# State-space groups: the products of the new inputs go ahead of the scaling of the former group's outputs, and the low part of those outputs goes to the end of its slot

## The chip, the cores and the metric

The kernel runs on one core of one Trainium2 chip. The metric is the device time of one execution in microseconds. TensorE (PE) multiplies matrices, VectorE (DVE) and ScalarE (ACT) work elementwise, GpSimd (POOL) helps, and SyncE (SP) issues the loads of weights.

## The reference, cut to what matters

A model of six layers on 256 tokens of 2048 numbers: four layers of attention and recurrence, then a state-space layer and a layer of dilated attention. Only the state-space layer (`_ssd_mixer`) is touched by the change. Its computation:

```python
z, xBC, dt = split(h @ in_w)
xBC = silu(causal_conv4(xBC) + conv_b)          # xs, B, C come out of this
dt = softplus(dt + dt_bias)
cb = C . B over the state, per group            # 8 groups of 8 heads of 64
decay = exp(acum_l - acum_s), causal
y_diag = (cb * decay) @ (xs * dt)
y = (y_diag + xs * D_skip) * silu(z)
y = y * rsqrt(mean(y*y over the group) + eps) * norm_g
out = y @ out_w                                  # 4096 -> 2048
```

There is one chunk of 256 tokens, so no state is carried from chunk to chunk.

## The kernel before, in words

**Products in three parts.** All values lie in SBUF with features on the 128 partitions and the 256 tokens along the free axis. Each fp32 weight is split into a high and a low part: ACT writes `w_hi` (line 1026), DVE writes `w_lo = w_raw - w_hi` (line 1594), and PE adds three products (lines 446 to 448). A load of weights is a *slot* of 16 blocks of 128x128, split in two halves of 1024 columns. There are two buffers of split weights, so the work of slot n on ACT and DVE (`hi_ahead`, `lo_half`) prepares the weights of slot n+2 in the buffer that PE frees half by half in slot n. PE writes its tiles to two banks in turn: a tile can start once DVE has taken the last tile but one (`tile_taken`).

**Groups.** `s_group(g)` runs 10 slots for each of the 8 groups, one tile each: slots 0 and 1 give B and C, slots 2 to 5 the four pairs of heads' inputs xs, and slots 6 to 9 the four tiles of z. After groups 2 and 4 comes a projection (`s_project`, 8 slots of two half-length tiles each), and after group 7 a third projection with `tail=True`, then the last one. Each engine's queue is written out by hand in this order; there is no planner, and each engine executes its own list in order, waiting on semaphores.

**What happens in a slot of a group.** DVE: low half 0, take the tile (line 2166), low half 1, then a piece of the former group (`s_previous`), in slots 4 to 7 the inputs of one pair (`s_inputs`: one product with D, line 2116, then four products of the turned tile with dt, line 2121, which release `turn_read`), then the convolution (slots 0 to 5, lines 2093 to 2096) and the clamp for the sigmoid (line 2103). ACT: high half 0, decays of a pair in slots 8, 9, 2 and 3 (`s_decay`, lines 1367 and 1370), high half 1, the sigmoid of the last slot's tile (lines 1070 to 1072), its piece of the former group, and in slot 7 two fetches of rows for the decays (`s_fetch`, line 1359, a DMA). POOL: the product with the sigmoid (line 2504), and the decays' product with cb (`s_weights`, lines 2511 and 2512), which releases `m_ready`. PE: the tile, then the former group's output product (`s_out`, lines 812 and 813, in slots 0, 1, 3 and 4, which waits for `m_ready` and for DVE's reading of the last one, lines 2109 and 2110), and in slots 4 to 7 the turn of a pair (`turn`, line 485, into one bank, which waits for `turn_read` of the last turn).

**The former group's outputs.** The four tiles of y are made in slots 0, 1, 3 and 4 (`s_y_out`), their squares are summed, the factor comes in slot 5, and in slot 6 DVE scales the four tiles (`s_scale_y`, line 2129). ACT then writes their high part (`s_y_hi`, line 1375) as the last thing of its slot 6, and DVE the low part (`s_y_lo`, line 2136) at the start of its slot 7. Only the projections read these.

Of the kernel before, what the change touches and what calls it, by code (L numbers as in the profile page):

```python
# [192 lines left out]
def _program(nc, ctx, t, counts):  # L193
# [91 lines left out]
    def K(name, n=None, rows=P):  # L285
        a = CON[name]
        w = dict(CONST_PARTS)[name] if n is None else n
        return con[0:rows, a:a + w]
# [1293 lines left out]
    def _(dve):  # L1582
# [6 lines left out]
        def lo_half(half, ahead=2):  # L1589

            k = c.k["slot"] + ahead - 1
            cols = slice(half * HALF, (half + 1) * HALF)
            dve.wait_ge(hi_ready, c.at("slot", ahead) * 2 + (half - 1) if half == 0 else c.at("slot", ahead) * 2)
            dve.tensor_tensor(w_lo[k % SPLIT][:, cols], raw[MAIN_AT[k] % RAW][:, cols], w_hi[k % SPLIT][:, cols], SUB).then_inc(lo_ready, 1)  # L1594

        def begin():

            c.next("slot")
            lo_half(0)
# [33 lines left out]
        def take(columns=False):  # L1633
            if columns:
                q = c.next("mod") - 1
                dve.wait_ge(ada_done, q + 1)
            dve.wait_ge(tile_done, c.next("tile"))
            g = G[c.bank][:, 0:SEQ]
            if columns:
                add = vec[:, VEC["ada_b"] + 2 * q:VEC["ada_b"] + 2 * q + 2]  # L1640
                dve.tensor_tensor(mod[:, 2 * q:2 * q + 2], G[c.bank][:, SEQ:SEQ + 2], add, ADD).then_inc(mod_done, 1)
            c.bank ^= 1
            return g
# [437 lines left out]
        def s_conv(g, n):  # L2081

            xb = s_xbp[:, n % 2]
            if n < 2:
                dst = s_bc[n]
                dve.wait_ge(cb_done, c.at("cb"))
                at = 32 + 8 * n + g
            else:
                dst = s_xv[n % 2]
                at = 4 * g + n - 2  # L2090
            dve.wait_ge(tile_taken, c.at("tile"))
            w = lambda k: V("s_conv_w", 48 * k + at)
            link(dve.tensor_scalar(dst, xb[:, 0:SEQ], w(0), V("s_conv_b", at), MUL, ADD))
            for k in (1, 2):
                link(dve.scalar_tensor_tensor(dst, xb[:, k:k + SEQ], w(k), dst, MUL, ADD))  # L2095
            link(dve.scalar_tensor_tensor(dst, xb[:, 3:3 + SEQ], w(3), dst, MUL, ADD))
            s_clamp(n, dst)

        def s_clamp(n, src):

            dve.wait_ge(gluon, c.at("glued", -1))
            c.next("glued")
            dve.tensor_scalar(s_zc[n % 2], src, SIG_MIN, None, MAX).then_inc(clamped, 1)

        def s_y_out(g, m):

            dve.wait_ge(yd_done, c.next("yd"))
            dve.wait_ge(gluon, 10 * g + 7 + m)
            link(dve.tensor_tensor(s_y[:, m], bO[:, 0:SEQ], s_dx[:, m], ADD))
            dve.tensor_tensor(s_y[:, m], s_y[:, m], s_z[:, m], MUL).then_inc(s_y_ready, 1)  # L2110

        def s_inputs(g, m):

            dve.wait_ge(gluon, c.next("gluon", 3 if m == 0 else 1))
            dve.wait_ge(s_y_ready, c.at("yd"))
            link(dve.tensor_scalar(s_dx[:, m], s_xv[m % 2], V("s_D", 4 * g + m), None, MUL))
            dve.wait_ge(turn_done, c.next("turn"))
            for b in range(2):
                for hh in range(2):
                    head = 8 * g + 2 * m + hh  # L2120
                    last = dve.tensor_scalar(s_xdt[:, b, m, 64 * hh:64 * hh + 64], bT[:, b * P + 64 * hh:b * P + 64 * hh + 64],  # L2121
                                             s_tok[:, b, head:head + 1], None, MUL)
            last.then_inc(turn_read, 1)

        def s_scale_y(g):

            factor()
            for m in range(4):
                last = dve.scalar_tensor_tensor(s_y[:, m], s_y[:, m], V("s_norm_g", 4 * g + m), rsn[:, 2], MUL, MUL)  # L2129
            last.then_inc(y_ready, 1)  # L2130
            dve.wait_ge(y_ready, c.next("y"))

        def s_y_lo(g):
            dve.wait_ge(x_hi, c.next("x"))
            four = slice(4 * (g % 4), 4 * (g % 4) + 4)
            dve.tensor_tensor(q_lo[:, four], s_y, q_hi[:, four], SUB).then_inc(x_lo, 1)

        def s_previous(g, step):
            if step in S_OUT:
                s_y_out(g, S_OUT.index(step))  # L2140
            if step == 6:
                s_scale_y(g)

        def s_steps(n):

            if n == 0:
                softplus_sum(s_y[:, 0], s_y[:, 1])
            if n == 1:
                softplus_end(s_dt[:], s_y[:, 0], s_y[:, 1], s_y[:, 2], s_y[:, 3], s_dt[:])
                link(dve.tensor_scalar(s_y[:, 0], s_dt[:], tiny[:, 0:1], -1.0, MUL, MUL))  # L2150
                link(dve.memset(s_y[:, 1], 1.0))
                dve.tensor_tensor_scan(s_ac[:], s_y[:, 1], s_y[:, 0], 0.0, MUL, ADD).then_inc(dt_ready, 1)
            if n == 4:
                dve.wait_ge(turn_done, c.next("turn"))
                dve.tensor_copy(s_tok.rearrange("p a b -> p (a b)"), bT[:]).then_inc(turn_read, 1)
                dve.wait_ge(turn_read, c.at("turn"))

        def s_group(g):
            for n in range(10):
                if g and n == 7:  # L2160
                    s_y_lo(g - 1)
                begin()
                if g == 0:
                    s_steps(n)
                x = take(columns=n == 1 and g in (3, 5))
                dve.tensor_copy(s_xbp[:, n % 2, 3:3 + SEQ] if n < 6 else s_z[:, n - 6], x).then_inc(tile_taken, 1)
                lo_half(1)
                if g:
                    s_previous(g - 1, n)
                if 4 <= n <= 7:  # L2170
                    s_inputs(g, n - 4)
                if n < 6:
                    s_conv(g, n)
                else:
                    dve.wait_ge(tile_taken, c.at("tile"))
                    s_clamp(n, s_z[:, n - 6])
                if n == 7:
                    dve.wait_ge(cb_done, c.next("cb"))
                    dve.tensor_tensor(s_cb[:, 0:P], bS[0][:, 0:P], K("causal"), MUL)
                    dve.tensor_copy(s_cb[:, P:SEQ], bS[0][:, P:SEQ])  # L2180
                    dve.tensor_tensor(s_cb[:, SEQ:384], bS[0][:, SEQ:384], K("causal"), MUL).then_inc(cb_read, 1)
            c.next("gluon", 4)
# [49 lines left out]
        def layer_s():  # L2232
            c.k["turn"] = 2 * 3 * A_HEADS + 3 * B_PAIRS
            dve.wait_ge(x_lo, c.at("x"))
            dve.sem_inc(mod_x, 1)
            link(dve.memset(s_xbp[:, :, 0:3], 0.0))

            begin()
            g = take()
            dve.tensor_scalar(s_dt[:], g, V("s_dt_bias"), None, ADD).then_inc(tile_taken, 1)  # L2240
            lo_half(1)
            dve.wait_ge(tile_taken, c.at("tile"))
            c.next("soft")
            softplus_begin(s_dt[:], s_y[:, 1])
            for g in range(S_GROUPS):
                s_group(g)
                if g in (2, 4):
                    s_project(g // 2 - 1)
            s_project(S_PAIRS - 2, tail=True)
            scale, gain = mod[:, 64:80], vec[:, VEC["ln_g"]:VEC["ln_g"] + DT]  # L2250
            dve.tensor_tensor(ln_a, gain, scale, MUL)
            link(dve.tensor_tensor(ln_b, vec[:, VEC["ln_b"]:VEC["ln_b"] + DT], scale, MUL))
            link(dve.tensor_tensor(ln_b, ln_b, mod[:, 48:64], ADD))
            s_project(S_PAIRS - 1)
            layer_norm(0)
# [544 lines left out]
```

## Time and profile before

| | us |
|---|---|
| median of 3 runs (3546.73 to 3554.34) | 3548.98 |
| profiled execution, its own time | 3549.42 |
| profiled execution, its span | 3547.6 |
| PE busy | 3447.0 (97%) |
| DVE busy | 2783.1 (78%) |
| ACT busy | 1987.5 (56%) |
| POOL busy | 587.2 (17%) |
| mean granted clock of TensorE | 0.995 |

The profiled execution is one run on the chip, recorded. A row of the timeline gives the start in us from the span's start, the length in us, the engine and line, the operation, and in brackets how long the engine had been idle before and what released it. Instructions of one line that follow one another are merged (x4), and their starts can overlap the end of the one before by some 0.09 us. The state-space layer lies between about 2216 and 2920 us. The rows below are mostly of group 3, whose slot 7 has its turn at 2507.30 on PE, and of group 4, which follows it directly. Groups 1 and 2, 3 and 4, and 5, 6 and 7 follow one another directly; the projections stand after groups 2, 4 and 7.

### The profile page before, as it was taken

The page shows a single profiled execution, that of the slowest core. Times are in us where ns is not written, and L with a number is a line of the kernel's source. Part 1 is how long each engine was busy: PE and PEld are TensorE (multiplying, and loading weights), DVE is VectorE, ACT ScalarE, POOL GpSimd, SP SyncE. Part 2 cuts the span into 40 slices and gives each one's busy share as a digit, 9 for nine tenths or more (in the row PEclk, how much of TensorE's full clock was granted, in tenths as well). Part 3 has the DMA queues.
Part 4 walks back from the last instruction along what each step waited for, and adds up shares of the span by engine and source line. Part 5 has one row for each costly group of instructions (what it writes and reads, how often), then busy time and mean ns, then how long its engine had stood idle before and what let it go on. Part 6 is the DMA issues. An engine that isn't in the chain of part 4 may idle for free.

```text
span 3547.6 us, 68240 instructions
## 1 busy us (share of the span) xinstructions
PE 3447.0 (97%) x27858; PEld 3381.8 (95%) x27858; DVE 2783.1 (78%) x4529; ACT 1987.5 (56%) x3204; POOL 587.2 (17%) x546
## 2 busy tenths in 40 slices
PE   7999999999999999999999999999999998999997
PEld 7999999999999998999999999999999998999997
DVE  7788888577797887877888887898989867666665
ACT  6555546566547676565555546665656746434344
POOL 2111112111113011131111112231313300000000
PEclk9999999999999999999999999999999999999999
DMA  6555556444465444655555565556464543555552
GB/s 239 217 197 219 217 227 231 176 155 179 165 251 203 172 169 173 267 185 218 201 221 202 208 262 180 178 175 230 171 233 169 186 169 146 210 189 199 204 190 107
DMA packets 113688, 699.61 MB, mean 197 GB/s; under 512 B 13216, under 2 KB 29792, under 8 KB 31456
## 3 DMA queue, kind: packets, MB, share of 16 engines
q1 hardware_dynamic: 104128, 685.14, 52.2%
q10 hardware_dynamic: 8784, 8.46, 1.0%
q8 instruction: 222, 3.64, 0.4%
q0 software_dynamic: 464, 1.64, 0.1%
q14 instruction: 90, 0.74, 0.1%
HBM read 684.64 MB, written 2.16 MB: 194 GB/s over the span
## 4 chain that ended last, share of the span: by engine, by line
PE 49%; DVE 13%; ACT 6%; issue 2%; DMA 1%; POOL 1%; DVEq 0%; SPq 0%; POOLq 0%; ACTq 0%
PE g L446 15%; PE g L448 15%; PE g L447 15%; DVE w_lo L1594 4%; ACT w_hi L1026 2%; DMA w_raw<-in_slots 1%; POOL scratch L2409 1%; DVE vec L2095 1%; DVE rstd L2095 1%; PE turn_bank L485 1%; DVE scratch L1659 1%; DVE scratch L2121 0%; DVE scratch L2129 0%; PE norm_bank L459 0%; DVE h L2225 0%
## 5 line engine op out<-in xcount | busy, mean ns | idle before, releaser
L1594 DVE TENSOR_TENSOR w_lo<-w_raw,w_hi 128x1024 fp32r<-128x1024 f32 x1088 | 1337.0, 1232 | 433.9 <-ACT w_hi L1026 423.1
L1026 ACT ACTIVATE w_hi<-w_raw 128x1024 fp32r<-128x1024 f32 x1088 | 1129.6, 1053 | 873.2 <-PE g L448 761.7
L446 PE MATMUL g<-p_hi,w_hi 128*128 128x256 f32 x4576 | 1318.0, 288 | 36.4 <-DVE w_lo L1594 23.2
L448 PE MATMUL g<-p_hi,w_lo 128*128 128x256 f32 x4576 | 1296.2, 283 | 0.0
L447 PE MATMUL g<-p_lo,w_hi 128*128 128x256 f32 x4576 | 1296.2, 283 | 0.0
L446 PE MATMUL g<-q_hi,w_hi 128*128 128x256 f32 x3408 | 980.0, 288 | 5.7 <-DVE w_lo L1594 2.2
L448 PE MATMUL g<-q_hi,w_lo 128*128 128x256 f32 x3408 | 964.0, 283 | 0.0
L447 PE MATMUL g<-q_lo,w_hi 128*128 128x256 f32 x3408 | 963.8, 283 | 0.0
L446 PEld LDWEIGHTS g<-p_hi,w_hi 128*128 128x128 f32 x4576 | 879.1, 192 | 46.1 <-DVE w_lo L1594 32.7
L447 PEld LDWEIGHTS g<-p_lo,w_hi 128*128 128x128 f32 x4576 | 879.3, 192 | 1.4
L448 PEld LDWEIGHTS g<-p_hi,w_lo 128*128 128x128 f32 x4576 | 879.0, 192 | 0.0
L446 PEld LDWEIGHTS g<-q_hi,w_hi 128*128 128x128 f32 x3408 | 653.1, 192 | 9.6 <-issue 3.5
L447 PEld LDWEIGHTS g<-q_lo,w_hi 128*128 128x128 f32 x3408 | 653.4, 192 | 1.1
L448 PEld LDWEIGHTS g<-q_hi,w_lo 128*128 128x128 f32 x3408 | 653.0, 192 | 0.0
L2409 POOL TENSOR_SCALAR scratch<-scratch 128x256 f32<-128x256 f32 x112 | 149.9, 1339 | 473.9 <-DVE scratch L1702 259.6
L2394 POOL TENSOR_TENSOR acc<-acc,sq 128x256 f32<-128x256 f32 x120 | 114.6, 955 | 306.5 <-ACT sq L1055 304.4
L1659 DVE SCALAR_TENSOR_TENSOR scratch<-w_raw,tiny,scratch 128x256 f32<-128x256 f32 x312 | 154.1, 494 | 8.6
L1070 ACT ACTIVATE scratch<-scratch 128x256 f32<-128x256 f32 x152 | 63.0, 414 | 166.4 <-POOL scratch L2409 165.0
L2449 POOL TENSOR_TENSOR scratch<-scratch,cos_a 128x256 f32<-128x256 f32 x64 | 52.6, 822 | 585.2 <-DVE scratch L1796 585.2
L1659 DVE SCALAR_TENSOR_TENSOR acc<-w_raw,tiny,acc 128x256 f32<-128x256 f32 x260 | 136.4, 525 | 7.1
L446 PE MATMUL g<-c_hi,w_hi 128*128 128x256 f32 x336 | 100.2, 298 | 0.4 <-DVE h L2186 0.4
L448 PE MATMUL g<-c_hi,w_lo 128*128 128x256 f32 x336 | 95.8, 285 | 0.0
(445 smaller groups left out, 3929.2 us busy)
## 6 DMA issues: line engine op xcount, KB each, us to landing
w_raw<-in_slots SPq DMA_DIRECT2D x640, 1024.0 KB, 4.9
scratch<-scratch SPq DMA_DIRECT2D x128, 64.0 KB, 4.9
scratch<-s_rows ACTq DMA_DIRECT2D x16, 256.0 KB, 3.4
con<-s_rows ACTq DMA_DIRECT2D x16, 256.0 KB, 5.1
h<-in_x SPq DMA_DIRECT2D x4, 512.0 KB, 6.2
out_h<-h SPq DMA_DIRECT2D x4, 512.0 KB, 2.6
sq<-in_p POOLq DMA_DIRECT2D x4, 256.0 KB, 3.0
con<-in_consts SPq DMA_DIRECT2D x1, 832.0 KB, 10.7
```

Source lines behind the costliest of these rows:

```text
L446: pe.matmul(g, wh, hi[:, k], start=n == 0, stop=False)
L447: pe.matmul(g, wh, lo[:, k], start=False, stop=False)
L448: last = pe.matmul(g, wl, hi[:, k], start=False, stop=n == len(ks) - 1)
L485: last = pe.transpose(bT[:, n * P:(n + 1) * P], s, K("ident"))
L1026: act.activation(w_hi[k % SPLIT][:, cols], raw[MAIN_AT[k] % RAW][:, cols], ACT.Copy).then_inc(hi_ready, 1)
L1070: link(act.activation(buf, buf, ACT.Exp, scale=-1.0))
L1594: dve.tensor_tensor(w_lo[k % SPLIT][:, cols], raw[MAIN_AT[k] % RAW][:, cols], w_hi[k % SPLIT][:, cols], SUB).then_inc(lo_ready, 1)
L1659: link(dve.scalar_tensor_tensor(a, w, s, a, MUL, ADD))
L2095: link(dve.scalar_tensor_tensor(dst, xb[:, k:k + SEQ], w(k), dst, MUL, ADD))
L2394: pool.tensor_tensor(acc[:], acc[:], sq[:, j % 2], ADD).then_inc(summed, 1)
L2409: pool.tensor_scalar(dst, src, SIG_MIN, None, MAX).then_inc(clamped, 1)
L2449: pool.tensor_tensor(t2[:, n % 2], qn[:, n % 2], cos_a[:], MUL).then_inc(cos_done, 1)
```

## The change

In the slots of groups 1 to 7 (where there is a former group):

- In slot 6 DVE runs the inputs of the third pair (`s_inputs`, 5 instructions) and the clamp first, and then the scaling of the former group's four tiles (`s_scale_y`).
- In slot 7 the low part (`s_y_lo`) is no longer before DVE's low half 0, but behind the clamp of the slot, ahead of the reading of the cb product.

In slots 0 to 5 the order is as before. The third projection (tail), ACT, POOL, PE and SP keep their lists.

```diff
         def s_group(g):
             for n in range(10):
-                if g and n == 7:
-                    s_y_lo(g - 1)
                 begin()
                 if g == 0:
                     s_steps(n)
                 x = take(columns=n == 1 and g in (3, 5))
                 dve.tensor_copy(s_xbp[:, n % 2, 3:3 + SEQ] if n < 6 else s_z[:, n - 6], x).then_inc(tile_taken, 1)
                 lo_half(1)
-                if g:
+                if g and n < 6:
                     s_previous(g - 1, n)
                 if 4 <= n <= 7:
                     s_inputs(g, n - 4)
...
                 else:
                     dve.wait_ge(tile_taken, c.at("tile"))
                     s_clamp(n, s_z[:, n - 6])
+                if g and n > 5:
+                    s_previous(g - 1, n)
+                if g and n == 7:
+                    s_y_lo(g - 1)
                 if n == 7:
                     dve.wait_ge(cb_done, c.next("cb"))
```

## Rows read from the trace of the kernel before

**Rows 1.** The waits of PE from 2200 to 2900: us in total, times, longest.
```profile
PE turn_bank L485 <- DVE scratch L2121: 9.6, 7, 1.4
PE out_bank L812 <- POOL scratch L2512: 3.0, 7, 0.8
```

**Rows 2.** The timeline of PE at slot 7 of group 3 and slot 3 of group 4.
```profile
2507.30 0.44 PE L485 MATMUL turn_bank<-con,vec 128*128 128x128 f32 x2 [1.37 <-DVE scratch L2121]
...
2545.28 0.66 PE L812 MATMUL out_bank<-scratch 128*64 128x256 f32 x4 [0.36 <-POOL scratch L2512]
```

**Rows 3.** The timeline of DVE, slots 5 to 8 of group 3.
```profile
2497.34 0.84 DVE L2116 TENSOR_SCALAR scratch<-vec 128x256 f32<-128x256 f32 x1
...
2503.80 2.16 DVE L2129 SCALAR_TENSOR_TENSOR scratch<-scratch,vec,rsn 128x256 f32<-128x256 f32 x4
2505.99 0.35 DVE L2116 TENSOR_SCALAR scratch<-rstd,vec 128x256 f32<-128x256 f32 x1
2506.38 0.86 DVE L2121 TENSOR_SCALAR scratch<-turn_bank,scratch 128x64 f32<-128x64 f32 x4
2507.16 0.28 DVE L2103 TENSOR_SCALAR scratch<-scratch 128x256 f32<-128x256 f32 x1
2507.36 1.22 DVE L2136 TENSOR_TENSOR q_lo<-scratch,q_hi 128x1024 fp32r<-128x1024 f32 x1
...
2516.62 1.23 DVE L1594 TENSOR_TENSOR w_lo<-w_raw,w_hi 128x1024 fp32r<-128x1024 f32 x1 [1.53 <-ACT w_hi L1026]
```

**Rows 4.** The scaling in the third projection, on DVE.
```profile
2875.86 1.67 DVE L2129 SCALAR_TENSOR_TENSOR scratch<-scratch,vec,rsn 128x256 f32<-128x256 f32 x4
```

**Rows 5.** The timeline of POOL in slot 6 of group 3.
```profile
2502.72 1.77 POOL L2504 TENSOR_TENSOR vec<-vec,sin_b 128x256 f32<-128x256 f32 x1 [4.69 <-ACT sin_b L1072]
```

**Rows 6.** The timeline of ACT, slots 6 to 8 of group 3, slots 0 to 2 of group 4.
```profile
2505.99 1.06 ACT L1375 ACTIVATE q_hi<-scratch 128x1024 fp32r<-128x1024 f32 x1 [3.35 <-DVE scratch L2129]
2506.96 1.99 ACT L1026 ACTIVATE w_hi<-w_raw 128x1024 fp32r<-128x1024 f32 x2
2509.74 0.37 ACTq L1359 DMA_DIRECT2D scratch<-s_rows  x1
...
2513.12 1.64 ACT L1367 ACTIVATE scratch<-scratch 128x128 f32<-128x128 f32 x4 [0.76 <-DMA scratch<-s_rows]
...
2524.81 1.99 ACT L1026 ACTIVATE w_hi<-w_raw 128x1024 fp32r<-128x1024 f32 x2
...
2535.84 0.42 ACT L1383 ACTIVATE rsn<-scratch 128x256 f32<-128x256 f32 x1 [1.13 <-DVE scratch L2110]
2536.32 1.06 ACT L1026 ACTIVATE w_hi<-w_raw 128x1024 fp32r<-128x1024 f32 x1
```

**Rows 7.** The timeline of DVE in slots 1 and 2 of group 4.
```profile
2533.54 1.23 DVE L1594 TENSOR_TENSOR w_lo<-w_raw,w_hi 128x1024 fp32r<-128x1024 f32 x1 [0.18 <-ACT w_hi L1026]
...
2540.77 1.23 DVE L1594 TENSOR_TENSOR w_lo<-w_raw,w_hi 128x1024 fp32r<-128x1024 f32 x1 [0.91 <-ACT w_hi L1026]
```

**Rows 8.** The timeline of DVE, slot 1 of groups 2, 6 and 7.
```profile
2355.54 1.23 DVE L1594 TENSOR_TENSOR w_lo<-w_raw,w_hi 128x1024 fp32r<-128x1024 f32 x1 [0.40 <-ACT w_hi L1026]
...
2711.61 1.23 DVE L1594 TENSOR_TENSOR w_lo<-w_raw,w_hi 128x1024 fp32r<-128x1024 f32 x1 [0.35 <-ACT w_hi L1026]
...
2777.08 1.23 DVE L1594 TENSOR_TENSOR w_lo<-w_raw,w_hi 128x1024 fp32r<-128x1024 f32 x1
```

**Rows 9.** DVE, then PE, at the third tile of the first projection.
```profile
2418.23 0.48 DVE L2186 SCALAR_TENSOR_TENSOR h<-g,mod,h 128x256 f32<-128x256 f32 x1
...
2418.61 0.28 PE L448 MATMUL g<-q_hi,w_lo 128*128 128x256 f32 x1
2418.86 0.36 PE L446 MATMUL g<-q_hi,w_hi 128*128 128x256 f32 x1
```

**Rows 10.** DVE, then PE, at the second tile of the third projection.
```profile
2835.96 0.47 DVE L2186 SCALAR_TENSOR_TENSOR h<-g,mod,h 128x256 f32<-128x256 f32 x1
...
2838.37 0.28 PE L446 MATMUL g<-q_hi,w_hi 128*128 128x256 f32 x1
```

## The prediction

> **What bounds the kernel now.** I read the busy shares first (PE 97%, DVE 78%, ACT 56%): PE sets the time, so an edit on DVE counts by what it does to PE's waits. Second, PE's waits in the state-space layer. Seven times, once in each of groups 1 to 7, the turn of slot 7 waits 1.37 us for DVE's products of slot 6, 9.6 us in all; seven more waits, 3.0 us, are for POOL's weights [rows 1]. Third, the timelines of the four engines around slot 7 of group 3. PE had its tile done at 2507.30 - 1.37 = 2505.93 and stood until L2121 ended at 2506.38 + 0.86 = 2507.24 [rows 2, 3]. DVE's list shows why: the scaling (L2129, 2.16 us) stands ahead of L2116 and L2121 [rows 3]. This is the wait that the change can take away.
>
> Fourth, who waits for the scaling. ACT's high part of y (L1375) stands idle 3.35 us for it, and behind it in ACT's queue lie the two high halves of slot 7, the sigmoid and the fetch of the rows at 2509.74 [rows 6]. The rows land at 2513.12, 3.38 us later, and ACT waits 0.76 us for them before the decays. From there to the pair of high halves that starts at 2524.81 ACT is all but always busy. DVE waits for ACT in slot 8 (1.53 us) and again in slots 1 and 2 of group 4 (0.18 and 0.91) [rows 3, 6, 7]. In slot 1 its output tile (L2110) releases ACT's square at 2535.84, behind which come the high half, the decays of pair 2 and the sigmoid; POOL's weights follow, and PE waits 0.36 us for them at 2545.28 [rows 2, 6]. After 2540.77 DVE has no wait until slot 8 of group 4. So end of scaling, fetch, decays, DVE in slots 0 and 1, ACT and DVE in slot 2, DVE to the next scaling form a ring with almost no slack, beside PE. That ring is the second bound, and the scaling's end lies on it.
>
> **The wait that goes.** After the change L2116 starts at 2503.80, where the scaling did. There it meets POOL's product (2502.72, 1.77 us) [rows 5]. In slot 5 the same instruction in the same position behind the low half took 0.84 us, against 0.35 in slot 6 [rows 3]. I take 0.84 + 0.03 to the next start. L2121 ends at 2503.80 + 0.87 + 0.86 = 2505.53, ahead of PE's 2505.93: the wait goes whole, 1.36 us a group (7 of them, 9.6).
>
> **The scaling's end.** L2116 0.87, four L2121 0.78 (2506.38 to 2507.16), the clamp 0.20 (to 2507.36), then four scalings. These took 2.16 us behind the low half but 1.67 in the third projection, where POOL runs nothing [rows 3, 4]; I take 1.67, since POOL's product is then over. The end moves from 2505.96 to 2503.80 + 3.52 = 2507.32: **s = 1.36 us later**. Bounds: nothing blocked, 0.39 + 0.78 + 0.20 + 1.67 - 2.16 = 0.88; both blocked, 1.85. The block of 0.49 moves from the scaling (2.16 - 1.67) to L2116 (0.84 - 0.35), so the middle value is the one that the rows fit.
>
> The Trainium skill, SBUF — State Buffer, "Who interferes with whom", says that a DVE instruction in a 2-port mode or with two SBUF inputs and a GpSimd one exclude each other for a whole instruction, whichever starts second. The trace agrees in kind (0.84 against 0.35). By that rule exactly one instruction pays, as in the middle value; without it s would be 0.88 and the sum below 2.5.
>
> **The low part of y.** L2136 (1.22 us) leaves the start of slot 7. Nothing on PE waits for it until a projection, more than two slots later. But DVE's low half 0 can't start at about 2508.5 any more: it needs ACT's high half, which now ends at 2506.96 + 1.36 + 1.04 = 2509.36, so DVE idles about 2.0 us and is 0.9 late. With L2136 behind the clamp (1.13) and up to 0.3 for a POOL product that L2116 of slot 7 now meets earlier, DVE is 2.3 us later at the second half of slot 8. It had idled 1.53 (1.6 with the overlap of starts) and ACT delivers 1.36 later, so 3.0 us are free [rows 3, 6]: the cover holds with 0.6 us to spare. PE's slots 8 and 9 need nothing earlier than that. So this half of the change costs nothing; if the cover goes, each further 0.1 us goes into the ring.
>
> **The lag, ring by ring.** ACT's high part, high halves, sigmoid and fetch all come s later; the fetch is issued at 2511.1 and lands at 2514.5. From there ACT, POOL and DVE carry s into slots 8, 9 and the next group. What absorbs it in a next group: the wait of DVE in slot 1 plus 0.09 of overlap, 0.49, 0.27, 0.44 and 0.09 for groups 2, 4, 6 and 7 [rows 7, 8] (in group 7 the low half has no wait before it), and ACT's gap between square and high half, 2536.32 against 2536.26 - 0.09, 0.15 [rows 6]. Together k = 0.65, 0.43, 0.59, 0.24. So PE, which waits for POOL's weights in slot 3 already, is there s - k later than before, although it comes 1.36 earlier: the wait grows from 0.36 to about 2.5 us and the gain is spent. Slot 7 then gives 1.36 back, but the ring is now s - k late, and the next scaling adds s once more.
>
> At a projection the lag reaches PE another way. Its fifth tile waits until DVE has taken the third: DVE takes it at 2418.23 to 2418.71, PE goes on at 2418.86, 0.13 behind its pitch [rows 9]. DVE has no wait between ACT's late high halves and this one, so PE takes over the whole lag there. It is the same after group 4. In the third projection DVE takes the second tile until 2836.43 and PE starts the fourth at 2838.37; less 0.15 from release to start, 1.8 us are free [rows 10]. Behind it DVE waits for PE several times, so nothing more is handed on.
>
> **The sum.** Groups 1 and 2 with the first projection: 2s - 0.65 = 2.07. Groups 3 and 4 with the second: 2s - 0.43 = 2.29. Groups 5, 6 and 7 with the third: 3s - 0.59 - 0.24 - 1.8 = 1.45. The removed waits are in this: these are PE's positions, and wherever PE waits for the ring its own earlier gain no longer counts. The sum is 7s - 3.71 = **+5.8 us**: 3549.42 + 5.8 = 3555.2 for an execution like the profiled one (span 3553.4), and 3554.8 against the median 3548.98, 0.44 below the profiled execution. With s = 0.88 it is +2.5, with 1.85 +9.2.
>
> **The rivals.**
> (a) *The wait goes and the lag is hidden*: -9.6 us, 3539.4. For it: PE is the 97% engine, and ACT and DVE show idle time in slot 8. Against it: that idle time is the ring's own (the rows' landing, then ACT), and is not there in slots 2 to 7. It needs 1.36 us of slack in the ring in each group; I find 0.24 to 0.65. 12%.
> (b) *The rings within the groups hold, but the projections swallow the lag*: PE leaves group 2 at 0.71 - 1.36 = -0.65, group 4 at -0.43, and the tail at +1.45, as above: +0.4, 3549.4. Against it is PE's late fifth tile [rows 9], a small wait of 0.13 us that might be something else. 16%.
> (c) *DVE itself becomes the bound in slots 7 and 8*: POOL's product, now 1.36 us later, blocks L2116 of slot 7 for most of its length, 1.1 us more than I take instead of the 0.6 to spare. Then 0.5 us more enter the ring in each of 7 groups, +3.5: 3558.3. It decides from an L2116 of 1.4 us on; the longest wait of this kind in these rows is 0.49. 12%.
>
> **The numbers.** My forecast has 60%, with (a) 12, (b) 16 and (c) 12. Within 0.2% (7.1 us; about what a measurement of this kernel can tell from no change) lie 3541.9 to 3556.1. My forecast is within but near the upper end; a quarter of its chance, 15, lies above it (s over 1.54, or less absorbed). So faster 12%, same 61% (45 + 16), slower 27% (15 + 12). The range 3546.5 to 3558.8 leaves out (a) and part of (c); my case alone has 3551.5 to 3558.2 from its bounds of s.
>
> **What would show it.** In the changed profile: PE's wait at L485 for L2121 gone in all seven groups; ACT's wait at L1375 3.35 + 1.36 = 4.7 us; PE's wait at L812 for POOL unchanged in groups 1, 3 and 5 and 2.4 to 2.9 us in groups 2, 4, 6 and 7; PE's wait for DVE's taking at the fifth tile of the first two projections about 2.9 us each (0.13 + 2.07 + 0.65, and 0.13 + 2.29 + 0.43); group 3's first slot 2.1 us later than now and group 5's 4.4. L812 waits that stay at 0.36 would prove me wrong at the ring, absent waits at L2186 at the projections, and a DVE that never waits for ACT in slot 8 would mean (c).

## The result and the profile after

The changed kernel takes 3555.59 us (median of 13 runs, 3553.19 to 3559.02) against 3548.87 of the kernel before (13 runs): +6.7 us, ratio 1.002 with a 95% interval of 1.0013 to 1.0027. Forecast were 3554.8 and +5.8. The profiled execution has a span of 3557.2 us. From the start of the last turn of dt in group 0 to the first matrix product of the layer norm behind the projections, the state-space layer took 2908.1 - 2237.6 = 670.5 us before and 2916.7 - 2240.0 = 676.7 after: 6.2 us more. The rest of the difference of the two spans (3.4 us) lies outside what the change touches.

PE's waits in the layer, us in total, times, longest:

```profile
PE out_bank L812 <- POOL scratch L2514: 9.7, 7, 2.3
PE g L446 <- DVE scratch L2164: 4.2, 3, 1.5
PE g L446 <- DVE h L2188: 3.2, 5, 1.1
...
PE out_bank L812 <- DVE scratch L2110: 1.0, 2, 0.9
```

The turn's wait of 9.6 us [rows 1] is gone: no row for L485 and L2121 is left. In its place the wait for POOL's weights grew from 3.0 to 9.7, and two waits for DVE's taking of tiles came: 4.2 us, and 3.2 where it had been 1.1. With 1.0 for DVE's output tile that is 14.0 us more and 9.6 less, 4.4 net. The remainder up to 6.2 is hardly idle time. For about 1.5 us it is TensorE's clock, which fell once in the layer, right behind the wait of 2.26 us in slot 3 of group 6. Each row gives a stretch, its length, the busy time of PE, PEld (the loading of weights), DVE, ACT and POOL, the granted clock, the DMA share and GB/s:

```profile
2720.00:2730.90 10.90, 8.65 (x73) 8.44 (x71) 9.87 (x15) 9.03 (x18) 5.43 (x5) 1.00 0.53 182
2730.90:2735.00 4.10, 4.10 (x23) 3.66 (x24) 4.03 (x8) 2.17 (x6) 1.82 (x2) 0.58 0.22 92
2735.00:2740.00 5.00, 5.00 (x44) 4.57 (x44) 4.86 (x7) 2.21 (x3) 2.71 (x3) 1.00 0.59 213
```

From 2732 to 2734 the granted clock is 0.50 (1.2 of 2.4 GHz). From the output product of slot 3 to that of slot 4 PE needs 2739.13 - 2730.90 = 8.23 us, against 2730.10 - 2723.35 = 6.75 before, 1.48 more. The waits of 2.23 and 2.25 us in groups 2 and 4 had no such fall behind them.

DVE in slot 6 and the start of slot 7 of group 3, then slot 8:

```profile
2508.27 0.83 DVE L2116 TENSOR_SCALAR scratch<-rstd,vec 128x256 f32<-128x256 f32 x1
2509.14 0.86 DVE L2121 TENSOR_SCALAR scratch<-turn_bank,scratch 128x64 f32<-128x64 f32 x4
2509.92 0.28 DVE L2103 TENSOR_SCALAR scratch<-scratch 128x256 f32<-128x256 f32 x1
2510.12 1.67 DVE L2129 SCALAR_TENSOR_TENSOR scratch<-scratch,vec,rsn 128x256 f32<-128x256 f32 x4
2513.92 1.22 DVE L1594 TENSOR_TENSOR w_lo<-w_raw,w_hi 128x1024 fp32r<-128x1024 f32 x1 [2.14 <-ACT w_hi L1026]
...
2522.97 1.23 DVE L1594 TENSOR_TENSOR w_lo<-w_raw,w_hi 128x1024 fp32r<-128x1024 f32 x1 [1.32 <-ACT w_hi L1026]
```

From the start of this piece to the scaling's end it is 2511.79 - 2508.27 = 3.52 us, against 2.16 before [rows 3]: the end is 1.36 us later, to the hundredth the s of the prediction. L2116 took 0.83 and the four scalings 1.67. DVE then idles 2.14 us for the high half, and in slot 8 it still waits for ACT (1.32), so it is not itself the bound there.

ACT in slots 6 to 8 of group 3:

```profile
2511.81 1.06 ACT L1375 ACTIVATE q_hi<-scratch 128x1024 fp32r<-128x1024 f32 x1 [4.71 <-DVE scratch L2129]
2512.78 1.99 ACT L1026 ACTIVATE w_hi<-w_raw 128x1024 fp32r<-128x1024 f32 x2
...
2515.56 0.37 ACTq L1359 DMA_DIRECT2D scratch<-s_rows  x1
...
2519.48 1.64 ACT L1367 ACTIVATE scratch<-scratch 128x128 f32<-128x128 f32 x4 [1.86 <-DMA scratch<-s_rows]
```

The high part waits 4.71 us where it had waited 3.35 [rows 6], and the chain behind it is the same. This fetch took 3.92 us to land instead of 3.38, so the decays begin half a us later than s alone would have it. Group 3 is the extreme: over groups 1 to 7 this landing took 3.10 to 3.92 us, against 3.13 to 3.55 before.

PE from slot 3 of group 2 on, waits for POOL, for DVE's output tile, and the new ones at the first projection:

```profile
2370.17 0.66 PE L812 MATMUL out_bank<-scratch 128*64 128x256 f32 x4 [2.23 <-POOL scratch L2514]
2413.08 0.39 PE L446 MATMUL g<-q_hi,w_hi 128*128 128x256 f32 x1 [1.54 <-DVE scratch L2164]
2419.61 0.39 PE L446 MATMUL g<-q_hi,w_hi 128*128 128x256 f32 x1 [0.42 <-DVE h L2188]
2423.33 0.36 PE L446 MATMUL g<-q_hi,w_hi 128*128 128x256 f32 x1 [0.58 <-DVE h L2188]
2484.28 0.66 PE L812 MATMUL out_bank<-scratch 128*64 128x256 f32 x4 [0.36 <-POOL scratch L2514]
2536.17 0.66 PE L812 MATMUL out_bank<-con,scratch 128*64 128x256 f32 x4 [0.88 <-DVE scratch L2110]
2550.99 0.66 PE L812 MATMUL out_bank<-scratch 128*64 128x256 f32 x4 [2.25 <-POOL scratch L2514]
...
2730.90 0.66 PE L812 MATMUL out_bank<-scratch 128*64 128x256 f32 x4 [2.26 <-POOL scratch L2514]
2797.30 0.66 PE L812 MATMUL out_bank<-scratch 128*64 128x256 f32 x4 [1.40 <-POOL scratch L2514]
```

Read it as a pattern: after a projection (2484.28, group 3) the wait is the old 0.36; in a group that directly follows another it is 1.4 to 2.3. From slot 3 of group 3 to slot 3 of group 4 PE needs 2550.99 - 2484.28 = 66.71 us. Before it was 65.46, so this group became 1.25 us longer although a wait of 1.37 had been taken out of it. It is the largest case: from group 1 to 2, 5 to 6 and 6 to 7 it is 65.88, 66.01 and 66.40, 0.4 to 0.9 longer.

### The profile page after: what moved, and what is told of

Read it like the earlier page. It is cut to its first block, busy times and chain, and to the rows that moved or that the text cites. A ratio compares the mean times of both kernels' runs of the same rounds, so it can differ in the third digit from the quotient of the medians.

```text
span 3557.2 us, 68247 instructions
## 1 busy us (share of the span) xinstructions
PE 3453.3 (97%) x27858; PEld 3389.3 (95%) x27858; DVE 2781.8 (78%) x4529; ACT 1985.4 (56%) x3204; POOL 586.4 (16%) x546
## 3 DMA queue, kind: packets, MB, share of 16 engines
HBM read 684.64 MB, written 2.16 MB: 193 GB/s over the span
## 4 chain that ended last, share of the span: by engine, by line
PE 44%; DVE 14%; ACT 8%; issue 3%; DMA 2%; POOL 1%; ACTq 0%; DVEq 0%; SPq 0%; POOLq 0%
PE g L446 13%; PE g L448 13%; PE g L447 13%; DVE w_lo L1594 5%; ACT w_hi L1026 3%; DMA w_raw<-in_slots 1%; DMA scratch<-s_rows 1%; POOL scratch L2411 1%; ACT scratch L1367 1%; DVE vec L2095 1%; DVE rstd L2095 1%; DVE scratch L1659 1%; PE turn_bank L485 1%; DVE scratch L2121 0%; DVE scratch L2164 0%
## 5 line engine op out<-in xcount | busy, mean ns | idle before, releaser
L446 PE MATMUL g<-q_hi,w_hi 128*128 128x256 f32 x3408 | 982.5, 288 | 11.5 <-DVE scratch L2164 4.2
```

The lines of the kernel that those rows point to most:

```text
L446: pe.matmul(g, wh, hi[:, k], start=n == 0, stop=False)
```

## The experiments

Each is timed against the kernel before in five rounds; changes in us are the difference of the medians, with the ratio's 95% interval. The changed kernel is called "after". The edits of experiments 1, 2, 5, 6, 7 and 9 are shown against the kernel before, those of 3, 4 and 8 against after.

**1. Only the scaling moved.** The low part of y stays at the start of slot 7.

```diff
-                if g:
+                if g and n < 6:
                     s_previous(g - 1, n)
...
                     s_clamp(n, s_z[:, n - 6])
+                if g and n > 5:
+                    s_previous(g - 1, n)
```

> Only the order of slot 6 is changed (inputs and clamp ahead of the scaling); the low part of y is at the start of slot 7 as before. My theory (a ring from the end of the scaling over ScalarE, the fetch of the rows, the decays and VectorE back to the next scaling, 1.36 us longer): the whole effect is in this half, +5 to +7 us against the kernel before, the wait of the turn in slot 7 gone, the waits for GpSimd's weights in slot 3 of groups 2, 4, 6 about 2.2 us. Rival (the moved low part of y makes VectorE late in slots 7 and 8, and that is the loss): -9.6 us here, since the turn's wait is gone and nothing else is added.

Measured: 3556.18 against 3549.67, +6.5 us, ratio 1.002 (1.0011 to 1.0029). PE's waits for POOL's weights are 10.4 us in seven, longest 2.3, and the turn's wait is gone. The whole loss is in this half.

**2. Only the low part moved.** Slot 6 is as before.

```diff
-                if g and n == 7:
-                    s_y_lo(g - 1)
                 begin()
...
                     s_clamp(n, s_z[:, n - 6])
+                if g and n == 7:
+                    s_y_lo(g - 1)
```

> Only the low part of y is moved behind the clamp of slot 7; slot 6 is as before. My theory: no change, -1 to +1 us; the turn's wait of 1.37 us stays in seven groups and VectorE idles a little more in front of its low half in slot 7 and less in slot 8. Rival (the low part's new place costs): +5 us or more.

Measured: 3547.90 against 3549.67, -1.8 us, ratio 0.9996 (0.9988 to 1.0005): not to be told from no change. The turn's wait is 9.5 us. The rival with the low part falls.

**3. After, with ACT's high part behind the fetch.** DVE's list is that of after.

```diff
-            if step == 6:
+            if step == 6 and g == S_GROUPS - 1:
                 s_y_hi(g)
...
                 if n == 7:
                     s_fetch(g, 0)
                     s_fetch(g, 1)
+                    if g:
+                        s_y_hi(g - 1)
```

> The changed kernel, and ScalarE's high part of y (which waits for the scaling) goes from the end of its slot 6 to the end of slot 7, behind the sigmoid and the fetch of the rows, for groups 1 to 7. The scaling's end is then off the ring. My theory: the gain of the turn's wait comes back whole, -8 to -10 us against the kernel before (about 15 faster than the changed kernel), the waits for GpSimd's weights in slot 3 back to about 0.4 us. Rival (VectorE's own list or its contention with GpSimd is what got longer): stays at +4 to +7 us, since VectorE's list is that of the changed kernel.

Measured: 3538.21 against 3549.67, -11.5 us, ratio 0.9971 (0.9960 to 0.9981), a little more than expected. It is 18 us under experiment 1 with the same slot 6 on DVE, so DVE's own list was not what cost. PE's waits in the layer, then its slot 3 in groups 3 and 4:

```profile
PE out_bank L812 <- POOL scratch L2516: 3.4, 7, 1.3
...
PE g L446 <- DVE h L2190: 1.1, 1, 1.1
```

```profile
2477.51 0.66 PE L812 MATMUL out_bank<-scratch 128*64 128x256 f32 x4 [0.36 <-POOL scratch L2516]
2541.40 0.66 PE L812 MATMUL out_bank<-scratch 128*64 128x256 f32 x4 [0.37 <-POOL scratch L2516]
```

Neither the turn's wait nor the new ones are there, and a group takes 63.89 us, 1.57 under the kernel before. I call the ring open here: the scaling's end no longer holds up ACT's high halves, the fetch and the decays, so it no longer leads back to itself. ACT in slots 7 and 8 of group 3 shows it:

```profile
2505.53 0.37 ACTq L1359 DMA_DIRECT2D scratch<-s_rows  x1
2505.94 0.48 ACTq L1359 DMA_DIRECT2D con<-s_rows  x1
2506.47 1.06 ACT L1375 ACTIVATE q_hi<-scratch 128x1024 fp32r<-128x1024 f32 x1 [0.52 <-issue]
...
2508.72 1.64 ACT L1367 ACTIVATE scratch<-scratch 128x128 f32<-128x128 f32 x4 [0.24 <-DMA scratch<-s_rows]
```

The high part waits for nothing but its place behind the fetch, and the decays wait 0.24 us instead of 1.86.

**4. After, with the fetches ahead of the high part.** The high halves still stand behind it.

```diff
+                if n == 6:
+                    s_fetch(g, 0)
+                    s_fetch(g, 1)
                 if g:
                     s_previous(g - 1, n)
-                if n == 7:
-                    s_fetch(g, 0)
-                    s_fetch(g, 1)
```

> The changed kernel, and ScalarE's two fetches of rows go from slot 7 to slot 6, ahead of the high part of y; the high part still holds the high halves. My theory: the ring's link over the fetch is cut, what is left of it (high part, two high halves, sigmoid, decays) ends 0.5 us before where it did in the kernel before, so the wait for the scaling is mostly covered: -4 to -8 us against the kernel before. Rival (the high halves behind the high part are the link that counts, not the fetch): no better than +3 us.

Measured: 3545.37 against 3549.67, -4.3 us, ratio 0.9989 (0.9980 to 0.9998). This is between the two theories, at the weak end of mine: by the medians, 11 us of after's lag and lost gain come back with the fetch, and 7 more only with experiment 3 (the profiled layers, 676.7, 669.7 and 659.6 us, have 7 and 10). The cause of the rest is in ACT's waits and PE's slot 3:

```profile
ACT q_hi L1375 <- DVE scratch L2129: 35.8, 8, 4.7
...
ACT sin_b L1070 <- DVE sin_b L2103: 12.9, 15, 1.6
```

```profile
2479.26 0.66 PE L812 MATMUL out_bank<-scratch 128*64 128x256 f32 x4 [0.36 <-POOL scratch L2514]
2544.39 0.66 PE L812 MATMUL out_bank<-scratch 128*64 128x256 f32 x4 [1.61 <-POOL scratch L2514]
```

The ring has a second way round, which I had not counted in full: ACT's own queue. Behind the high part it runs its high halves, sigmoids and decays of slots 7 to 9 without a wait, and at the last sigmoid it waits 1.56 us for DVE's clamp of slot 9 (0.3 before), because DVE's low half and clamp there take 1.95 and 0.83 us beside POOL's products (weights, then the one with the sigmoid), against 1.23 and 0.29 before. From the high part to that last sigmoid it is 16.75 us (2506.80 to 2523.55), against 18.14 in after (2511.81 to 2529.95) and 17.60 before. The fetch gives back 1.4 us of the ring and no more, and a group takes 65.13 us where PE with the ring open needed 63.89.

**5. The scaling's end late, the turn's wait kept in part.** Three scalings ahead of the inputs, the fourth behind the clamp.

```diff
-        def s_scale_y(g):
+        def s_scale_y(g, first=0, end=4):
...
-            factor()
-            for m in range(4):
+            if not first:
+                factor()
+            for m in range(first, end):
...
+            if end == 4:
+                last.then_inc(y_ready, 1)
...
-                s_scale_y(g)
+                s_scale_y(g, 0, 4 if g == S_GROUPS - 1 else 3)
...
                     s_clamp(n, s_z[:, n - 6])
+                if g and n == 6:
+                    s_scale_y(g - 1, 3)
```

> From the kernel before: in slot 6 of groups 1 to 7 three of the four scalings stay ahead of the inputs and the fourth, which releases ScalarE's high part, goes behind the clamp. The end of the scaling is then as late as in the changed kernel, while the turn of slot 7 still waits some 1.0 of its 1.37 us. My theory (only the end of the scaling counts, the removed wait is worth next to nothing): +5 to +7 us against the kernel before, as in the changed kernel. Rival (the two effects add, the lag costs some 16 us and the removed wait gives 9.6 back): +10 us or more.

Measured: 3554.82 against 3547.93, +6.9 us, ratio 1.0016 (1.0008 to 1.0025), the same as after. PE's waits:

```profile
PE out_bank L812 <- POOL scratch L2516: 8.9, 7, 2.1
PE turn_bank L485 <- DVE scratch L2121: 5.0, 6, 0.8
```

The scaling ends 3.51 us behind the low half of slot 6 (2504.56 to 2508.07 in group 3), as late as in after (3.52). 5.0 us of the turn's wait are still there and the kernel is as slow as with none. With the ring closed, the removed wait was worth nothing.

**6. The old order of slot 6, the ring open.** Low part and high part late, as in experiments 2 and 3.

```diff
-            if step == 6:
+            if step == 6 and g == S_GROUPS - 1:
                 s_y_hi(g)
...
+                    if g:
+                        s_y_hi(g - 1)
...
-                if g and n == 7:
-                    s_y_lo(g - 1)
                 begin()
...
+                if g and n == 7:
+                    s_y_lo(g - 1)
```

> From the kernel before: the scaling stays ahead of the inputs in slot 6, the low part of y goes behind the clamp of slot 7, and ScalarE's high part behind the fetch of slot 7 (as in e3_high_late). The ring is open, and the turn's wait of 1.37 us stays. My theory: -3 to 0 us, since PE's own waits are what bounds it then; with e3_high_late this gives the removed wait its price of 8 to 10 us once the ring is open. Rival (the earlier high halves, fetch and decays are what made e3_high_late fast, not the turn's wait): -8 us or more.

Measured: 3546.88 against 3547.93, -1.1 us, ratio 0.9996 (0.9987 to 1.0005). The turn's wait stands at 9.4 us. An open ring alone brings nothing measurable; with it the order of slot 6 is worth some 10 us (experiment 3).

**7. The fetches early, in the kernel before.** The move of experiment 4 without the change on DVE.

```diff
+                if n == 6:
+                    s_fetch(g, 0)
+                    s_fetch(g, 1)
                 if g:
                     s_previous(g - 1, n)
-                if n == 7:
-                    s_fetch(g, 0)
-                    s_fetch(g, 1)
```

> From the kernel before: only the two fetches of rows go from slot 7 to slot 6, ahead of the high part of y. My theory: -2 to +1 us; the decays no longer wait for rows, but the turn's wait stays and bounds PE. Rival (the landing of the rows is itself what bounds the kernel before): -4 us or more.

Measured: 3549.52 against 3547.93, +1.6 us, ratio 1.0005 (0.9996 to 1.0014). No change; in its profile the turn's wait is 9.4 us. The landing of the rows did not bound the kernel before.

**8. Experiments 3 and 4 together.**

```diff
-            if step == 6:
+            if step == 6 and g == S_GROUPS - 1:
                 s_y_hi(g)
...
-                if n == 7:
+                if n == 6:
                     s_fetch(g, 0)
                     s_fetch(g, 1)
+                if g and n == 7:
+                    s_y_hi(g - 1)
```

> The changed kernel with ScalarE's high part in slot 7 and the fetches in slot 6. My theory: the ring is open by e3_high_late alone, so this adds little: -10 to -13 us against the kernel before, within 1.5 us of e3_high_late. Rival (the landing of the rows, 4.8 us of waits in e3_high_late, still holds PE): -15 us or more.

Measured: 3536.25 against 3547.93, -11.7 us, ratio 0.9963 (0.9951 to 0.9976), the fastest here; experiment 3 is not clearly behind. PE's waits for POOL's weights are 2.5 us in seven, 0.4 at most, and no wait of the decays for rows is left.

**9. The new order only ahead of the projections** (groups 2 and 4). The low part of y is late in all groups, as in experiment 2; that piece is not shown.

```diff
-                if g:
+                if g and (n < 6 or g not in (2, 4)):
                     s_previous(g - 1, n)
...
+                if g in (2, 4) and n > 5:
+                    s_previous(g - 1, n)
```

> The new order of slot 6 only in groups 2 and 4, the ones directly ahead of a projection; all other groups keep the old order there; the low part of y is late in all groups (which costs nothing by e2_low_only). My theory (the lag of 1.36 us reaches PE whole at the fifth tile of the projection and spends the removed wait): +1.36 us for each of the two, +2 to +3.5 us against the kernel before, PE's waits of some 2.8 us behind each of the two turns. Rival (the projections swallow the lag, the loss of the changed kernel is all between groups): -2.7 us.

Measured: 3550.86 against 3547.62, +3.2 us, ratio 1.001 (1.0000 to 1.0019). The rival's -2.7 lies outside. PE at the first projection:

```profile
2406.64 0.39 PE L446 MATMUL g<-q_hi,w_hi 128*128 128x256 f32 x1 [1.28 <-DVE scratch L2164]
2413.19 0.39 PE L446 MATMUL g<-q_hi,w_hi 128*128 128x256 f32 x1 [0.45 <-DVE h L2188]
2416.89 0.36 PE L446 MATMUL g<-q_hi,w_hi 128*128 128x256 f32 x1 [0.57 <-DVE h L2188]
```

A projection hands the lag to PE, but by three waits rather than one, and the first and largest is at its second tile, which needs the bank of slot 9's tile.

## Why the prediction was right

**The wait that goes.** Right, in all seven groups. Its price was a little low. The prediction took 1.37 us a group from the idle time ahead of PE's matmul, which is counted from the modelled end of the product before. From start to start it was 2507.30 - 2505.65 = 1.65 us before and is 2510.25 - 2510.13 = 0.12 in after, 1.53 less. Once nothing else held PE, a group got 1.57 shorter (experiment 3), and the layer 670.5 - (2897.8 - 2238.2) = 10.9 us against 9.6. PE's waits ahead of the loading of weights had that number already: 11.0 us, 7 times, longest 1.6 in the kernel before.

**The scaling's end.** Right to the hundredth (3.52 us; the block by POOL moved from the scaling to L2116: 0.83 and 1.67). The rule of the Trainium skill that the prediction weighed (SBUF — State Buffer, "Who interferes with whom": the later one waits for the whole instruction) agrees, since one instruction paid and not both. Experiments 1 and 5 show that it is this end, and neither the removed wait nor the low part, that sets the time.

**The low part.** Right: it cost nothing (experiment 2), in slot 8 DVE still waits for ACT, 0.5 to 1.3 us in all seven groups, and L2116 of slot 7 took 0.83 or 0.84 us where rival (c) needs 1.4. Rival (c) is refuted.

**The lag, ring by ring.** The mechanism is shown by experiment 3, where the same list on DVE is fast once the high part no longer stands before ACT's high halves and fetch. The Trainium skill (PSUM — Partial Sum Buffer, "Engine vs sequencer instructions") calls ScalarE's queue strictly first in, first out, and the trace agrees: the high half starts at 2512.78, right behind the high part, although PE had begun the turn of slot 7, which stands behind the whole tile that this half waits for, at 2510.25. The sizes by PE's place in slot 3, less what it was before at the same place and less the 2.46 us by which this execution already was later at the layer's start: group 2 2370.17 - 2367.28 - 2.46 = +0.4 (0.7 predicted); group 3 2484.28 - 2479.82 - 2.46 = +2.0 (2.1); group 4 +3.3 (3.0); group 5 +4.5 (4.4); group 6 +5.1 (5.1); group 7 +6.0 (6.3). At the end, 2889.01 against 2880.49, +6.1 (5.8). The waits in slot 3 were 2.2 to 2.3 in groups 2, 4 and 6 where 2.4 to 2.7 follow from the prediction. In groups 4 and 6 DVE's output tile in slot 1 now held PE too (0.88 and 0.17), which the prediction had left out; in group 2 the lag itself was 0.3 smaller. In group 7 the wait was 1.40 where 2.8 had been said: PE had lost 1.48 us by the fall of its clock in group 6 and came that much later (1.40 + 1.48 = 2.88). So the fall cost next to nothing at the end: the ring, not PE, set the place of group 7. The prediction did not ask what longer waits do to the clock.

**The projections.** The lag reached PE whole, as predicted, and experiment 9 shows it alone (+3.2 for two; 2.7 by the sum). The place was wrong: the prediction put one wait of 2.9 us on the fifth tile. The runs show 1.54, 0.42 and 0.58 in after, at the second, fourth and fifth tile; in the third projection, too, the first wait (1.36, by the same release) is there, and not at the fourth tile. The sum of the three is 2.5, so the total was hardly touched. In the third projection the prediction let 1.8 us of the lag be covered; by the positions it was about 6.0 + 1.36 - 6.1 = 1.3 (an estimate from the numbers above).

**What was missed without harm.** The ring's second way, over ACT's queue alone (experiment 4), is 1.4 us shorter than the way over the fetch, and so never showed while the fetch was the longer one. It is why that experiment came out at the weak end of its -4 to -8.

**Luck in the number.** The forecast of +5.8 lies within the measured +4.6 to +9.6 (the interval), and PE's places bear the terms out within 0.3 us up to group 7. That the end agrees as closely is in part luck: a lag 0.3 us smaller at group 7 and a cover 0.5 us smaller in the third projection nearly cancel, and the fall of the clock happened where the ring hid it.

Open in part: experiment 4's median gained 4.3 us while its profiled layer (2905.7 - 2236.0 = 669.7) is only 0.8 shorter than the one before. Of the difference, 1.5 us are the clock: in this execution it was 0.59 from 2244.5 to 2248.0, behind PE's wait of 1.92 us for DVE in group 0, and two turns lie 7.51 us apart there, 6.02 in the kernel before. The same fall stands in the profiles of experiments 1, 5, 6, 7 and 9 and not in those of before, after, 2, 3 and 8, behind a wait of the same length, so profiled layers compare to some 1.5 us only. For the rest, the interval of experiment 4 reaches from 0.7 to 7 us.

Open too: how much of after's spread between groups is the landing time of the rows. The four groups that follow another took longer in the order of the landing in the group ahead of each (65.88, 66.01, 66.40 and 66.71 us for 3.10, 3.20, 3.35 and 3.92), but no experiment held it fixed.

## What to carry to other kernels

Before moving work ahead of a release, ask what is queued in order behind the instruction that waits for that release; here one elementwise copy that nobody needed soon held back the weights, the fetch and the decays of everything after it. Here a wait of the busiest engine was worth its size only once a ring of the other engines no longer had nearly the same period: look for a chain that comes back to itself, and compare its length with the engine's own. The repair was on another engine than the change: with the waiting copy put behind the urgent work, the same order gave 11 us instead of costing 7.

## What the runs showed of the hardware

The stop of PE at the transposition of slot 7 cost more than its idle row says: 1.37 us idle before the matmul, 1.6 before its weight load, and 1.57 came back when it was gone (65.46 to 63.89 us a group, experiment 3).

TensorE's granted clock fell to half (0.50) for some 3 us behind some of PE's waits and not behind others of the same length: behind 2.26 us in group 6 of after, not behind 2.23 and 2.25 in groups 2 and 4; behind 1.9 us in group 0 in six of the eleven profiles. Each of these falls cost 1.5 us of PE's time, and no row of waits shows it.

The fetch of 256 KB of rows, by ScalarE's queue, landed after a median of 3.4 us before and 4.0 after for the same 16 issues (4.0 in experiments 1 and 5, 3.7 in 4, 3.2 to 3.4 in the others). What sets it is not shown. A chain that goes through a DMA takes it over.
